# Delta rule: the 32x32 block inverses made on DVE within the input product, q and k normed there, and the remaining conditioning weights brought through the ring beside the heads

## The reference, cut to what matters

```
qkv = silu(causal_dwconv(h @ w_in[:, :3072], conv_w));  z = next 1024 columns;  a, bt = last 16 columns
q = l2norm(q) * dk**-0.5;   k = l2norm(k);   beta = sigmoid(bt);   g = -exp(a_log) * softplus(a + dt_bias)
gc = cumsum(g) in a chunk;  decay[i, j] = exp(gc[i] - gc[j]) for i >= j
kk = strictly lower part of (beta * k) k^T * decay
[u, w] = (I + kk)^-1 [beta * v, beta * exp(gc) * k]          # triangular solve in each chunk
v_new = u - w S;   o = (q * exp(gc)) S + (q k^T * decay) v_new
S = S * exp(g_last) + (k * exp(g_last - gc))^T v_new          # from chunk to chunk
out = (rmsnorm(o) * norm_w * silu(z)) @ w_out
mod = silu(c @ cond_w + cond_b) @ ada_w[0] + ada_b[0]         # six vectors of 1024
```

## Time and profile before

| | |
|---|---|
| Median of 3 runs | 3570.9 us (3568.86 to 3576.98) |
| The profiled execution itself | 3567.3 us |
| Its span, first to last instruction | 3565.8 us |
| TensorE busy | 3116.5 us (87%) |
| Mean granted TensorE clock | 0.925 of full speed |
| DVE, ACT, POOL busy | 1119.9, 796.2, 883.6 us |

### The profile page before, as it was taken

One profiled execution on the slowest core, in us unless ns is written; L12 is line 12 of the kernel. 1 busy time (PEld: TensorE's weight loads), 2 busy tenths in 40 slices (PEclk: granted clock), 3 DMA queues, 4 the chain that ended last, 5 costly groups with the idle time before them and its releaser, 6 DMA issues. The chain is left out here.

```text
span 3565.8 us, 45694 instructions
## 1 busy us (share of the span) xinstructions
PE 3116.5 (87%) x18594; PEld 2057.4 (58%) x18594; DVE 1119.9 (31%) x1876; ACT 796.2 (22%) x1138; POOL 883.6 (25%) x743
## 2 busy tenths in 40 slices
PE   6997876999989998899998968899788888888887
PEld 3774764788768875678776957345333333333333
DVE  3524426656244005332304166442301101111111
ACT  1224333222232223222314252111100000000001
POOL 1430113444435331344442314000011111111110
PEclk9997778999999999999998988899899999999999
DMA  6316002455312330222331202103599999999997
GB/s 222 94 48 236 3 3 79 148 174 191 81 66 82 107 94 12 83 83 94 100 89 54 83 14 70 51 0 129 219 409 412 423 408 406 414 412 406 403 399 280
DMA packets 246198, 631.10 MB, mean 177 GB/s; under 512 B 18693, under 2 KB 191782, under 8 KB 220785
## 3 DMA queue, kind: packets, MB, share of 16 engines
q1 hardware_dynamic: 235249, 618.68, 46.1%
q0 software_dynamic: 10240, 8.43, 0.8%
q10 hardware_dynamic: 576, 2.10, 0.1%
HBM read 633.33 MB, written 20.97 MB: 183 GB/s over the span
## 5 line engine op out<-in xcount | busy, mean ns | idle before, releaser
L418 POOL TENSOR_TENSOR ring_parts<-ring,arena_parts 128x512 fp32r<-128x512 f32 x544 | 708.1, 1335 | 1156.2 <-ACT arena_parts L394 1001.2
L526 PE MATMUL ps<-arena_parts,arena_parts 128*128 128x512 f32 (+1 forms) x2080 | 786.7, 378 | 95.1 <-POOL ring_parts L418 52.4
L528 PE MATMUL ps<-arena_parts,ring_parts 128*128 128x512 f32 (+1 forms) x2080 | 774.9, 373 | 0.0
L3555 PE MATMUL ps<-arena 128*64 128x512 f32 x1024 | 516.6, 663 | 158.9 <-DMA arena<-in_w_up 114.8
L527 PE MATMUL ps<-hT_parts,arena_parts 128*128 128x512 f32 (+1 forms) x1728 | 632.5, 366 | 0.0
L3556 PE MATMUL ps<-arena 128*64 128x512 f32 x1024 | 518.0, 665 | 0.0
L526 PEld LDWEIGHTS ps<-arena_parts,arena_parts 128*128 128x128 f32 x2080 | 399.5, 192 | 188.1 <-issue 53.0
L528 PEld LDWEIGHTS ps<-arena_parts,ring_parts 128*128 128x128 f32 x2080 | 399.9, 192 | 71.7
L3555 PEld LDWEIGHTS ps<-arena 128*64 128x64 f32 x1024 | 150.2, 152 | 494.0 <-issue 492.1
L527 PEld LDWEIGHTS ps<-hT_parts,arena_parts 128*128 128x128 f32 x1728 | 331.6, 192 | 51.4
L394 ACT ACTIVATE arena_parts<-ring 128x2048 fp32r<-128x2048 f32 (+1 forms) x105 | 210.7, 2007 | 410.1 <-PE ps L528 368.0
(11 more groups left out here) (523 smaller groups left out, 3658.6 us busy)
## 6 DMA issues: line engine op xcount, KB each, us to landing
arena<-in_w_down SPq DMA_DIRECT2D x64, 2048.0 KB, 23.5
arena<-in_w_gate SPq DMA_DIRECT2D x63, 2048.0 KB, 18.4
arena<-in_w_up SPq DMA_DIRECT2D x63, 2048.0 KB, 22.8
ring<-in_ffn_up SPq DMA_DIRECT2D x44, 1024.0 KB, 5.1
arena<-in_ada_w SPq DMA_DIRECT2D x20, 2048.0 KB, 9.8
ring<-in_ret_w_in SPq DMA_DIRECT2D x24, 1024.0 KB, 5.2
ring<-in_ffn_down SPq DMA_DIRECT2D x16, 1408.0 KB, 6.9
ring<-in_gdn_w_in SPq DMA_DIRECT2D x16, 1024.0 KB, 5.8
```

Source lines behind the costliest of these rows:

```text
L418: ins = pool.tensor_tensor(lower[:, at], whole[:, at], upper[:, at], ALU.subtract)
L526: pe.matmul(out, upper[:, r], self.upper[r][:, part], start=(r == 0), stop=False)
L528: ins = pe.matmul(out, lower[:, r], self.upper[r][:, part], start=False, stop=(r == self.tiles - 1))
L3555: pe.matmul(k.ps[upper, 2 + u, :], m.xeT[u][:, r, :], m.w_up[u][:, r, :], start=(r == 0), stop=(r == KD - 1))
```

## The change

- **Norm stage gone.** Its meeting is gone too (`base` 13 instead of 14, and the stage numbers that SP waits for are one lower).
- **Input product.** The product's chunks are written out without loops, with one counter for all 32 tiles. The order of tiles is k first, then q, then v. Beside the products TensorE, at places fixed by the dictionaries `beside`, turns the gate rows, sums the squares of k and q (`sums`: four tiles share one bank by 32-row windows), spreads each inverse root over the partitions (`spread`: a column of the identity as weights, taken with step 0, and two rounded parts), and forms the 32x32 grams of k (`gram`: 16 matmuls a head). ACT adds squares, roots and decays; DVE adds the gate columns, differences, strengths and the products with the inverse root (`unit`).
- **Inversion.** `invert` (below) makes the inverses of all 128 blocks at once on DVE by forward substitution, in PSUM banks 4 and 5, four blocks of 32 partitions by 32 systems, and transposes them into `X` and `XT`.
- **Heads.** `first` and `inner` with their masks are gone, `LEVELS` is 2. `join` reads `X` and `XT` of the input stage; POOL places the diagonal blocks (`diagonal`) earlier. Corners stand first on ACT, keys of both next heads behind the last `new`, in front of the output copies.
- **Conditioning weights.** `RingConditioning` takes the last four parts in 16 chunks of 256 columns through the ring, five chunks a pair (one in the last), each with its row product on TensorE and its sum on DVE. TensorE waits for DVE's sum (`added`) in each place. The column sums stand in the last pair in front of `whole_dx`.
- **xT** is scaled by DVE in the last pair.

```
+    def invert(self, dve, st):
+        k, n = self.k, self.SUB
+        of = lambda b: k.ps[:, b:b + 2, :].rearrange("p b c -> p (b c)")
+        X = of(self.INVERSE).rearrange("p (i c) -> p i c", c=n)
+        self.early.wait(dve, "gram", 1)
+        st.done(dve.transpose(self.lower.rearrange("p j i -> p i j"), of(self.SYSTEM).rearrange("p (b i) -> p i b", i=n)))
+        self.norm.wait(dve, "inverted", 2 * GH)
+        st.done(dve.memset(X, 0.0))
+        st.wait()
+        st.done(dve.tensor_tensor(self.lower, self.lower, self.decay, ALU.mult))
+        st.done(dve.memset(of(self.INVERSE)[:, 0:n * n:n + 1], 1.0))
+        st.wait()
+        for j in range(n - 1):
+            shape = [P, n - 1 - j, j + 1]
+            term = self.step[:, j % 2, 0:shape[1] * shape[2]].rearrange("p (i c) -> p i c", c=j + 1)
+            st.done(dve.tensor_tensor(term, X[:, j, 0:j + 1].unsqueeze(1).to_broadcast(shape), self.lower[:, j, j + 1:].unsqueeze(2).to_broadcast(shape), ALU.mult))
+            st.wait()
+            st.done(dve.tensor_tensor(X[:, j + 1:, 0:j + 1], X[:, j + 1:, 0:j + 1], term, ALU.add))
+            st.wait()
+        dve.wait_ge(k.sem("gdn_silu"), self.BANKS + self.CONVOLVED)
+        dve.transpose(self.X.rearrange("p (b c) -> p c b", c=n), X.rearrange("p i c -> p c i"))
+        dve.transpose(self.XT.rearrange("p (b i) -> p i b", i=n), X)
...
+        beside = {7: [(turn_gates,)], 6: [(sums, 0, 0)], 10: [(sums, 0, 1)], 14: [(sums, 1, 0)], 18: [(sums, 1, 1)]}
+        for n in range(GH):
+            beside.setdefault(14 + n // 2, []).append((spread, 0, n))
+            beside.setdefault(22 + n // 2, []).append((spread, 1, n))
+            beside.setdefault(18 + n, []).append((gram, n))
...
+        beside = {9: [(gate_columns,), (differences,)], 13: [(split_root, 0)], 21: [(key_scale,), (split_root, 1), (strengths,)]}
...
+        beside = {12: [(root, 0)], 20: [(root, 1), (decays,)]}
+        for n in range(GH):
+            for kind in range(2):
+                beside.setdefault(kind * GH + n + self.LAG, []).append((square, kind, n))
...
         for p in range(GH // 2):
             more, a, b = p < GH // 2 - 1, 2 * p + 2, 2 * p + 3
+            join_t1(p)
             if more:
                 spread_g(a)
+                spread_b(a)
+            if p:
+                added(5 * p - 1)
+            join_dx(p)
             if more:
                 spread_g(b)
+                spread_b(b)
+            whole_t1(p)
+            rows(5 * p)
             if more:
                 gram_k(a)
+            added(5 * p)
+            if not more:
+                self.cond.tensor_sums(pe)
+            whole_dx(p)
             if more:
                 gram_k(b)
             keys(p)
             for t in range(GCN):
                 values(p, t)
+                if more:
+                    rows(5 * p + t + 1)
+                if more:
+                    (gram_q, gram_q, turn_k, turn_k)[t]((a, b)[t % 2])
+                    if t < GCN - 1:
+                        added(5 * p + t + 1)
                 states(p, t)
+                if more and t == GCN - 1:
+                    turn_v(a)
                 outputs(p, t)
+            if more:
+                turn_v(b)
```

More of the change, by code:

```diff
@@ L787, in __init__, with tile_of @@
         self.w_gate = room.take(KD, 2 * GH)
+        self.pick = k.as_parts(room.take(P))
         self.head = room.take(2, 1)
         self.rows = room.take(4, T)
+        cells = self.rows.rearrange("p b t -> p (b t)")
+        self.decay, self.lower = (cells[:, n * D:(n + 1) * D].rearrange("p (j i) -> p j i", i=self.SUB) for n in range(2))
+        self.cols = room.take(2, self.SUB)
+        self.window = room.take(2 * self.SUB)
+        self.step = room.take(2, 2 * P)
+        z = lambda n, m=1: self.tiles[:, 3 * GH + n:3 * GH + n + m, :]
+        self.square = z(0, 4)
+        self.root = z(4)[:, 0]
+        self.norm = Signals(k, "norm", squared=2 * GH, summed=4, rooted=4, inverted=2 * GH)
+        self.early = Signals(k, "heads", spread=2 * GH, gram=1, diff=1, exp=1)
+        self.parts = Signals(k, "input", rounded=2, split=2)
+        self.root_parts = [k.as_parts(z(5 + n)[:, 0]) for n in range(2)]
+    def tile_of(self, g):
+        return 2 * self.ORDER[g // 2] + g % 2 if g < self.CONVOLVED else g
     def sync(self, sp):
@@ L800, in sync @@
             (self.blocks, k.tables["t_blocks"])])
[L801 removed]
+        for c in range(NSLOT, self.CHUNKS):
+            chunk(c)
+        self.stream.n += self.CHUNKS
     def tensor(self, pe, stream):
@@ L812, in tensor @@
         pe.sem_inc(k.sem("gdn_convolved"), self.BANKS)
[L813 to L825, removed]
@@ L836, in tensor, with turn_gates, sums @@
-        ins.then_inc(k.sem("gate_cols"), 1)
+        def turn_gates():
+            pe.wait_ge(k.sem("gate_rows"), 5)
+            for what, rows in enumerate((self.g_rows, self.b_rows)):
+                for t in range(GCN):
+                    at = (what * GCN + t) * GH
+                    ins = pe.transpose(k.ps[:, self.TURN, at:at + GH], rows[:, t * P:(t + 1) * P], k.ident[0:GH, 0:GH])
+            ins.then_inc(k.sem("gate_cols"), 1)
+        def sums(kind, batch):
+            self.norm.wait(pe, "squared", kind * GH + 4 * batch + 4)
+            if kind and batch == 0:
+                self.norm.wait(pe, "rooted", 1)
+            for q in range(4):
+                ins = pe.matmul(k.ps[q * self.SUB:(q + 1) * self.SUB, self.SUMS, :], self.window[:, self.SUB - 1 - batch:2 * self.SUB - 1 - batch],
+                                self.square[:, q], start=(batch == 0), stop=(batch == 1))
+            ins.then_inc(self.norm.sem("summed"), 1)
@@ new lines, in spread @@
+        def spread(kind, n):
+            at = self.SUB * (n % 4) + n // 4
+            bank = self.SPREAD[n % 2] if kind == 0 else self.SPREAD[0] - n % 2
+            if n == 0:
+                self.parts.wait(pe, "split", kind + 1)
+            if n >= 2:
+                self.norm.wait(pe, "inverted", kind * GH + n - 1)
+            pick = self.pick[:, at:at + 1].to_broadcast([P, P])
+            pe.matmul(k.ps[:, bank, :], pick, self.root_parts[0], start=True, stop=False)
+            pe.matmul(k.ps[:, bank, :], pick, self.root_parts[1], start=False, stop=True).then_inc(self.early.sem("spread"), 1)
@@ new lines, in gram @@
+        def gram(h):
+            self.norm.wait(pe, "inverted", GH)
+            out = k.ps[:, self.SYSTEM:self.SYSTEM + 2, :].rearrange("p b c -> p (b c)")
+            for t in range(GCN):
+                for r in range(4):
+                    at, to = t * GC + r * self.SUB, (t * GH + h) * self.SUB
+                    key = self.tiles[:, GH + h, at:at + self.SUB]
+                    ins = pe.matmul(out[r * self.SUB:(r + 1) * self.SUB, to:to + self.SUB], key, key, start=True, stop=True)
+            if h == GH - 1:
+                ins.then_inc(self.early.sem("gram"), 1)
@@ L1413, in scalar @@
                 new(p, t)
-                if more and t < 2:
-                    keys(a + t)
+            if more:
+                keys(a)
+                keys(b)
             for h in (2 * p, 2 * p + 1):
```

487 lines of the change are left out of this document (255 added, 232 removed).

## The result

The changed kernel takes 3475.9 us (median of 4 runs, 3472.2 to 3477.9) against 3571.5 us for the kernel before in the same series (4 runs, 3568.9 to 3577.0): a ratio of 0.9728, 95% interval 0.9717 to 0.9740. The forecast was 3473 us, between 3440 and 3503. The profiled execution took 3474.4 us, its span 3472.6; the sum had made it 3469.

A forecast was written before the change was run, and what follows sets the result against it. Stage lengths count: input product bound by TensorE, norm stage by transfers, heads a chain. -56.1 + 9 - 51 = -98 us takes the profiled 3567.3 to 3469, the median to 3473; range 3440 to 3503.

The forecast's parts named there:

- Norm stage -56.1, input product +9: Removing the norm stage saves 56.1 us; work moved into the input product makes TensorE end there at 277 instead of 268.
- The inversion: DVE's 62 steps in the input product take 23.2 us, 29.4 with surrounding work, hidden behind the z tiles at no cost.
- My bound above: Upper case for DVE's inversion: 0.34 us fixed a step, 38.7 us in all, 3.2 late.
- No register in the convolution: Input product: convolution steps, 0.90 us apart, need no register; set against ACT's added square, 0.2 us a pair, 1.5 us.
- The claim on tile 20: Input product: ACT's root and decays at tile 20 take some 6 us, with cover of 2 us before TensorE would wait.
- Heads -51: Heads stage falls from 201.6 to 150.5 us: 14 in front, 111 for three pairs, 25.5 for the last.
- A pair of 37: A middle pair of heads takes 37 us against 47: TensorE's work 30.6 us plus waits of 6.
- Low clock: Rival: new waits keep TensorE's clock low in the heads, pairs of 44 to 46 us, total 3500; chance 0.2.
- The inversion as bound: Rival: at 0.7 us a step DVE's inversion takes 61 us, ending 25 late in the input product, total 3498; chance 0.07.
- Grams of the dear form: Rival: the input product's small grams cost 0.29 us each, 37 us instead of 5.1, total 3501; chance 0.03.
- Straight-line code: Rival: sequencers fall behind on the input product's written-out rounds, 31 us, total 3504, chance 0.03; slower than before 0.02.
- Shorter pairs of 33: Rival: heads all at the higher clock with ends overlapping, 33 us a pair, 136 in all, total 3459; chance 0.15.

The follow-up runs named there:

- the probes: Changed kernel with the inversion's 62 steps replaced by three copies and three block transposes of 1024 elements on DVE; one execution took 3473.3 us.
- the gram moved: Changed kernel with the second head's key gram on TensorE behind the pair's key products instead of in front; 3464.8 us, ratio 0.9702.

## Why the prediction was right, and where its terms were off

- *Norm stage -56.1, input product +9.* Right: -47.0 measured for -47.1, with luck in the parts. (The terms listed add to 9.6.) From the convolution of tile 2 to the end of tile 31 it is 179.1 us; 29 tiles at 5.54 are 160.7, so the extras take 18.4, against 16.2 and the 0.7 that the gates' transposes took before. TensorE ends at 277.4 (forecast 277), 9.0 later than before, of which 0.9 already stand ahead of tile 2's convolution (98.33 instead of 97.39) and have nothing to do with the sum. The wait of 3.7 us on DVE is gone. Waits on POOL fell less than I had it: 2.6 us (2.1 of it one wait at the start) against 3.7 over the stretch of the earlier trace rows, -1.1 for -1.8; from tile 2 on it is 0.4 against 1.5.
- *The inversion.* Start 244.4 (244), chain 23.5 us (23.2). Around it 8.6 us instead of 6.2: the three transposes take 2.1, not 1.25 (the probes: the strided view). A step that writes PSUM is 0.01 us longer than the one before it that writes SBUF. Cover 3.3 us, shown by the doubled chain, where my sum had 6. It was hidden, but with half the margin. My bound above was too low: 0.90 us less 512 elements at 1.04 ns leave 0.37 fixed, not 0.34, and 40.4 us, not 38.7.
- *No register in the convolution.* Its second step now starts 0.78 us behind the first instead of 0.90. In the trace of before a register instruction of 0.06 us stands on DVE ahead of each such step (it doesn't count as busy), and now there is none. The square on ACT in exchange cost nothing visible. The claim on tile 20 held as well: DVE waited 0.23 us for ACT there.
- *Heads -51.* Right in kind, 7 us too much: 157.6 instead of 150.5. The step that was mis-sized is the part in front of the first pair, 18.5 instead of 14. I took DVE's compact products off the old 17.1 and overlooked that join_dx now waits for ACT, which has 16 key copies (4.0 us) and four corners (1.3) ahead of it; in the kernel before the doubling ran meanwhile. That wait is 2.5 us, and the run with ACT's keys in another order, where it is gone, has 15.9 in front. Most of the other 1.9 us is a term that was too large: I took off 3.1 for DVE's compact products and the masks, where TensorE had waited 1.5 us for DVE in that stretch before. The pairs sum to 112.3 (111), the last stretch is 26.8 (25.5), as the column sums run at the lower level.
- *A pair of 37: two errors that cancel.* TensorE is busy 33.2 us on average instead of 30.6, since some 13, 18 and 13 us of the pairs are at the lower level (from the clocks 0.82, 0.77 and 0.82); the chunks alone take 6.2 us (1.93 and four of 1.07) instead of 4.6. And it waits 4.3 instead of 6: 1.7 (2.5) for the output copies, 1.7 (1.9) for the second head's differences, 0.5 (0.7) for w. My mark of 3 us for the keys was not reached.
- *The rivals.* Low clock: half there (0.82, 0.77 and 0.82 against my "above 0.8"), without the pairs of 44 to 46. My bound of 180 us for the heads was no bound: 30.6 us half as long again are 45.9, and with the waits of 6 a pair would take 52, not 45. The inversion as bound: out, by 3.3 us. (Grams of the dear form would have added 37 less 5.1, so 3505 and not 3501.) Straight-line code: over the stretch of the earlier trace rows TensorE's weight loads of L526 waited 4.1 us for nothing visible, against 9.9. Shorter pairs of 33 came true only with the gram moved.
- *By the sum*: 3469 forecast, +7.1 in the heads, +0.1 up to them, -1.9 behind them make the 3474.4 measured. The 1.9 are no part of the forecast; without them it would have been 7 us low instead of 5.

## What to carry to other kernels

A chain of small dependent DVE instructions could be priced from another such chain in the same trace (23.2 us for 23.5) and hidden behind TensorE; double it once to learn the cover that is left. Where the profile shows a stretch at the lower clock, a short wait of TensorE inside it or just ahead of it can cost more than its length, here 3.5 us a pair for 2.2 of waits, and that gap is where to try real work first. An order that shortens a wait but does not close it can measure as nothing and still be needed. And ask who waits next for what was moved back: ACT's new order took a wait of 2.5 us from the front and put 1.5 behind it.

## What the hardware showed that was not expected

- *Clock.* In the versions with almost the same matmuls (all but the two that move or halve the chunks' work) a pair's mean clock lay between 0.77 and 0.95. With gaps of 1.7, 1.1 and 0.7 us ahead of the 32x32 and 8-row matmuls the lower level took 9 to 18 us of a pair. In the second and third pair it took 3.4 us with idle products in the gap (0.4 us left), with a chunk in it 6.8, and with a second chunk and its wait of 0.54 us 10 and 14. Shown is that filling the gap raises the clock, even with products that serve nothing. Which of the matmuls behind the gap bring it down is open, and so is why the second chunk did not help.
- *DVE strides.* 1024 f32 elements read from PSUM take 1.25 us in order and 2.1 us with a stride of 32 elements on both sides (copy and transpose alike). One of the two transposes at the end (L1083) reads in order and writes to SBUF with that stride, and takes 2.06 too, so the strided write is enough; a strided read alone no run has. The Trainium skill (Vector Engine (DVE) Microarchitecture Reference, "The reshape front-end and per-opcode configuration") has a 32x32 transpose keep up one element per cycle and lane; the probes in order agree (1.25 us for 1024), and what I had missed lay in the view, not in the operation.
- *DVE's fixed part.* The steps of 31 elements last 0.19 us and start 0.23 apart. The Trainium skill (VectorE: DVE Perf Modes, "The TRN2 errata") gives 151 cycles fixed, 0.157 us at its 0.96 GHz. An estimate by it for 31 elements, at the 1.04 ns of the router's rows, is 0.19 us, so the durations agree, and 0.03 us between dependent instructions come on top, 2.1 us over the 62 steps.
